# Six gate/up chunks of the first feed-forward half as seven block products, with their forms made earlier

## The chip, the cores and the metric

The kernel runs on one core of a Trainium2 chip. The metric is the device time of the program in microseconds (us), the median of several executions. Times "from the span's start" are those of one profiled execution, counted from its first instruction.

## The reference

The program is a block of a hybrid model on 528 tokens (16 meta tokens and 512 of the sequence) of width 1024: a feed-forward layer, a mixer (latent attention and a gated delta rule), a second feed-forward layer, and then a second block with two more attention branches. The change is in the first feed-forward layer alone:

```
D_FF = 2816
def rmsnorm(x, w):
    x32 = x.astype(jnp.float32)
    y = x32 * lax.rsqrt(jnp.mean(x32 * x32, axis=-1, keepdims=True) + EPS)
    return (y * w.astype(jnp.float32)).astype(x.dtype)
def swiglu(x, w_gate, w_up, w_down):
    return (jax.nn.silu(x @ w_gate) * (x @ w_up)) @ w_down
...
h = h + 0.5 * swiglu(rmsnorm(h, ffn1_norm[l]), ffn1_w_gate[l], ffn1_w_up[l], ffn1_w_down[l])
```

## The kernel before

**Precision.** Each product of two float32 matrices is made of three matmuls (`mm3`, L745 to L747): every operand is split into a high part (`WHI`, `UH`, `FH`, `GH`) and a low part, the difference (`WLO`, `UL`, `FL`, `GL`), and high x high, low x high and high x low are summed in PSUM. ScalarE makes a high part (a copy in the rounded type), VectorE the low part (source minus high).

**The stream of weights.** All weights come as chunks in one fixed order (`STREAM`), through two slots (`RAW[:, slot]`, slot = n % 2): SP loads chunk n, ScalarE makes `WHI` (`hi_part`, L1542), VectorE `WLO` (`lo_part`, L2125), TensorE multiplies and counts `mm_done`, VectorE reads PSUM and counts `evac`. The feed-forward layer takes two halves of 11 x 128 hidden columns: f1u0 (gate/up chunks n = 0 to 10, each the gate and the up columns of 128 hidden ones, 16 blocks of 128 x 128), f1d0 (down chunks 11 to 18, 11 blocks each), f1u1 (gate/up 19 to 29), f1d1 (down 30 to 37). Every engine has its own instruction queue and works through it in order; the helper `stream` calls a body per chunk, as a hardware loop of two chunks per turn, or straight (`straight=True`).

**A plain gate/up chunk** is 96 matmuls of 128 x 128 by 264 tokens (8 blocks of the width, gate and up, two token halves, three precision products). In its body (`up`), ScalarE and VectorE first make the weights of chunk n + 1 (`next_hi`, `next_lo`). Then they wait for chunk n's product: VectorE multiplies the gate by the row factors (L2351), ScalarE takes tanh (L1678), VectorE makes silu (L2353), multiplies by the up part out of PSUM (L2358, which counts `evac`) and by the row factors (L2361), ScalarE makes `GH` (L1680), VectorE `GL` (L2363).

**A seven-product chunk** (`seven_products`, `seven_up`; chunks 19 to 29) does the same product by Strassen's seven block products: the width, the hidden columns of gate and up, and the tokens are each cut in two. Seven combinations of the normed inputs are needed ("forms", 128 x 1056 each, `FH` and `FL`, made once) and seven combinations of the weights ("pieces" of 128 x 512, made per chunk: two sums for the lower half, `lower_sums`, two more in `piece_low`, and then high and low of each of the seven). A product is 12 matmuls of 264 tokens, so a chunk is 84. Some products are wanted in two outputs: ScalarE copies a PSUM half bank into another (`forked`, L1609, counts `snap`) or to `SNAP` (`copied`, L1616), TensorE waits for such copies before products 2, 4 and 6, and VectorE adds twice at the end. Pieces live in a ring of eight places in the two weight slots.

**The forms** are made in the down chunks 11 to 17 (`normed_inputs`, `forms`, `form_high`): eight normed halves (L2164), two differences (L2173, L2176) and seven low parts (L2187, L2185) by VectorE, seven high parts (L1563) by ScalarE, two sums by POOL (L639, L641). TensorE waits for all seven (`f_lo`) before the first product of the first seven-product chunk.

**Memory.** `FH`, `FL`, `XB` (the forms before the split) and `UH0`, `UL0` (the plain normed inputs) share an arena by their life times.

Of the kernel before, what the change touches and what calls it, by code (L numbers as in the profile page):

```python
# [17 lines left out]
P = 128  # L18
# [4 lines left out]
HT = T1 // 2  # L23
# [4 lines left out]
FP = 272  # L28
# [51 lines left out]
def build(nc, io):  # L80
# [44 lines left out]
    def region(start, *items):  # L125
# [14 lines left out]
    FH, FL, SNAP, SX, TANH1, SILU1, GF1, GH, GL, _ = region(  # L140
        arena, ("FH", [P, 7, 4, FP], f32r), ("FL", [P, 7, 4, FP], f32r), ("SNAP", [P, 1, HT], f32),
        ("SX", [P, PIECE], f32), ("TANH1", [P, 2, T1], f32), ("SILU1", [P, 2, T1], f32), ("GF1", [P, 2, T1], f32),
        ("GH", [P, FHALF, T1], f32r), ("GL", [P, FHALF, T1], f32r))
    XB, _ = region(arena + size([P, 7, 4, FP]), ("XB", [P, 8, 4, FP], f32))
    UH0, UL0, _ = region(arena, ("UH0", [P, KD, T1], f32r), ("UL0", [P, KD, T1], f32r))
# [300 lines left out]
    SEVEN_RUNS = (range(START["f1u1"], START["f1u1"] + FHALF),)  # L446
# [8 lines left out]
    FORM_HI = (0, 1, 5, 2, 3, 4, 6)  # L455
# [15 lines left out]

    def piece_place(t, n, i):

        where = RING[(7 * (n - SEVEN_FIRST[n]) + i) % 8]
        return t[:, where // 4, where % 4 * PIECE:(where % 4 + 1) * PIECE]

    def piece_free(eng, n, i):

        q = 7 * (n - SEVEN_FIRST[n]) + i
        if q < 8:  # L480
            eng.wait_ge(mm_done, SEVEN_FIRST[n] - (1 if q < 4 else 0))
        else:
            eng.wait_ge(p_mm, 7 * SEVEN[SEVEN_FIRST[n]] + q - 7)
# [10 lines left out]
    def hidden(f):  # L494
        return (GHS, GLS) if f else (GH, GL)
# [77 lines left out]
    def _(sp):  # L573
# [40 lines left out]
        for name in ORDER[:-1]:  # L614
            stream(sp, name, load(name), straight=name == "f1u1", first=2 if name in ("f1d0", "f1d1") else 0)
            if name == "z":
                spread_rows()
# [122 lines left out]
    def _(pe):  # L740
# [13 lines left out]
        def square_sums(v):  # L754
# [59 lines left out]
        def down_by_halves(n, slot, gh, gl):  # L814

            for half in range(2):
                if half:
                    pe.wait_ge(evac, n)
                for k in range(FHALF):
                    if half == 0:  # L820
                        pe.wait_ge(gl_rdy, 3 * FHALF + k + 1)
                    a = HS * half
                    last = mm3(PS[:, 1 - half, 0:HS], slot, k * P, gh[:, k, a:a + HS], gl[:, k, a:a + HS],
                               k == 0, k == FHALF - 1)
# [25 lines left out]
        def ffn(f, c0, w):  # L850
            hi, lo = parts(3 * f)
            gh, gl = hidden(f)
            for half in range(2):
# [27 lines left out]
                def down(n, j, turn, slot, nxt):  # L881
                    pe.wait_ge(lo_rdy, n + 2)
                    pe.wait_ge(evac, n - 1)
                    if last_down(f, half, j):
                        down_by_halves(n, slot, gh, gl)
                        return
                    for k in range(FHALF):
                        pe.wait_ge(gl_rdy, (2 * f + half) * FHALF + k + 1)
                        for b, (a, m, c) in enumerate(pieces(w)):
                            last = mm3(PS[:, 4 * slot + b, c:c + m], slot, k * P, gh[:, k, a:a + m],  # L890
                                       gl[:, k, a:a + m], k == 0, k == FHALF - 1)
# [4 lines left out]
                stream(pe, f"f{f + 1}u{half}", up, straight=f == 0 and half == 1, first=2)  # L896
# [633 lines left out]
    def _(act):  # L1530
# [24 lines left out]
        def form_high(i):  # L1555
# [5 lines left out]
            else:  # L1561
                act.wait_ge(xn_rdy, 4 if i == 0 else KD)
# [48 lines left out]
        def copied(n):  # L1611
# [3 lines left out]
            act.wait_ge(comb, 2 * c)  # L1615
            A(SNAP[:, 0, :], bank_half(n, 1), ACT.Copy).then_inc(snap, 1)  # L1616

        def hidden_high(n, q, j):

            act.wait_ge(evac, n + 1)  # L1620
            A(GH[:, j, :], GF1[:, q % 2, :], ACT.Copy).then_inc(gh_rdy, 1)

        def seven_up(n, j, q, nxt):
# [7 lines left out]
            if first:  # L1631
# [15 lines left out]
            if not last:  # L1647
# [8 lines left out]
        def ffn(f, c0, w):  # L1656
            TANH, SILU, GF = staging(f)
            for half in range(2):
                m0 = f * FJ + half * FHALF - START[f"f{f + 1}u{half}"]

                def up(n, j, turn, slot, nxt):
# [18 lines left out]
                    A(hidden(f)[0][:, j, 0:w], GF[:, slot, 0:w], ACT.Copy).then_inc(gh_rdy, 1)  # L1680

                def down(n, j, turn, slot, nxt):
                    next_hi(n, turn, slot, nxt)
                    if f == 0 and half == 0:
                        for i in {2: FORM_HI[:3], 3: FORM_HI[3:5], 4: FORM_HI[5:]}.get(j, ()):
                            form_high(i)
# [6 lines left out]
                stream(act, f"f{f + 1}u{half}", up, straight=f == 0 and half == 1, first=2)  # L1693
                stream(act, f"f{f + 1}d{half}", down, straight=f == 0 or half == 1)
# [20 lines left out]
        for k in range(KD):  # L1715
            A(SQ[:, k, :], H[:, k, :], ACT.Square).then_inc(sq_rdy, 1)
# [394 lines left out]
    def _(dve):  # L2111
# [32 lines left out]
        def lower_sums(n):  # L2144
# [45 lines left out]
        def hidden_low(q, j):  # L2190

            dve.wait_ge(gh_rdy, q + 1)
            TT(GL[:, j, :], GF1[:, q % 2, :], GH[:, j, :].bitcast(f32), ALU.subtract).then_inc(gl_rdy, 1)

        def seven_up(n, j, q, nxt):
# [6 lines left out]
            else:  # L2202
                hidden_low(q - 1, j - 1)
            if last:
# [13 lines left out]
            if not last:  # L2218
# [11 lines left out]
            else:  # L2230
# [59 lines left out]
        def normed_inputs(j):  # L2290

            if j == 0:
                dve.wait_ge(mm_done, FHALF)
            for k in range(4 * j, 4 * j + 4) if j < 2 else ():
                normed_halves(k)
# [32 lines left out]
        def ffn(f, c0, w):  # L2328
            gh, gl = hidden(f)
            TANH, SILU, GF = staging(f)  # L2330
            for half in range(2):
# [3 lines left out]
                def up(n, j, turn, slot, nxt):  # L2335
# [6 lines left out]
                    elif n == 0:  # L2342
                        lo_part(2, 0, SLOT)
                    if f == 1:
# [18 lines left out]
                    TT(gl[:, j, 0:w], GF[:, slot, 0:w], gh[:, j, 0:w].bitcast(f32),  # L2363
                       ALU.subtract).then_inc(gl_rdy, 1)

                def down(n, j, turn, slot, nxt):
# [12 lines left out]
                    if f == 0 and half == 0:  # L2379
                        normed_inputs(j)  # L2380
# [4 lines left out]
                    if f == 0 and half == 0:  # L2385
                        forms(j)
# [949 lines left out]
```

## Time and profile before

| | us |
|---|---|
| median of 3 runs (1556.37 to 1559.57) | 1557.88 |
| the profiled execution | 1557.85 |
| its span, first to last instruction | 1556.2 |
| TensorE busy | 1519.9 |
| VectorE busy | 955.3 |
| ScalarE busy | 593.6 |

The profiled execution's mean granted TensorE clock is 0.997. Busy time of TensorE is that of pipelined instructions, which overlap: one row of 0.28 us for a matmul of 264 tokens does not mean that it holds the engine for that long; the distance from one to the next does.

### The profile page before, as it was taken

Reading aid. Unit: us, or ns where it says so; the run is one execution under the profiler, and the core shown is the slowest. Engines: PE = TensorE matmul, PEld = TensorE weight load, DVE = VectorE, ACT = ScalarE, POOL = GpSimd, SP = SyncE. Lnnn points to the kernel's source line nnn. Section 1 sums busy time; section 2 is a strip of 40 time slices with the busy share of each in tenths; the row PEclk is TensorE's granted clock in tenths of the full one; section 3 lists DMA queues with packets and bytes.
Section 4 is the critical chain, followed back from the end, with each engine's and each line's share of the span. In section 5 each row is a group of like instructions: output and inputs, shape, how many; then the busy total and the mean of one; then the engine's idle time right before and its main releaser. Section 6 shows DMA issues by size and latency. Waiting matters only on the chain.

```text
span 1556.2 us, 30392 instructions
## 1 busy us (share of the span) xinstructions
PE 1519.9 (98%) x12676; PEld 1334.2 (86%) x12676; DVE 955.3 (61%) x1528; ACT 593.6 (38%) x968; POOL 127.0 (8%) x124
## 2 busy tenths in 40 slices
PE   9999999999999989999999989999999989999998
PEld 8999999999997779988888868888888877776777
DVE  6546588855389776546345666634666565557872
ACT  6222356632255562043223312212222143446960
POOL 0000100000001640500000000000000000000410
PEclk9999999999999999999999999999999999999999
DMA  6222223246332200012224243333342353211001
GB/s 242 81 99 75 92 100 109 92 114 145 96 85 70 61 3 31 5 42 81 94 90 166 82 162 127 131 119 123 134 153 76 106 213 135 76 47 55 2 13 71
DMA packets 27679, 147.85 MB, mean 95 GB/s; under 512 B 2928, under 2 KB 3328, under 8 KB 16944
## 3 DMA queue, kind: packets, MB, share of 16 engines
q1 hardware_dynamic: 21616, 122.50, 22.5%
q0 software_dynamic: 5424, 22.68, 5.3%
q8 instruction: 84, 1.38, 0.4%
q10 hardware_dynamic: 528, 1.08, 0.2%
q14 instruction: 27, 0.22, 0.0%
HBM read 140.97 MB, written 5.27 MB: 94 GB/s over the span
## 4 chain that ended last, share of the span: by engine, by line
PE 87%; DVE 7%; ACT 3%; issue 2%; DMA 1%; POOL 1%; DVEq 0%; SPq 0%; ACTq 0%; POOLq 0%
PE PS L745 22%; PE PS L746 22%; PE PS L747 22%; PE PS L845 2%; PE PS L847 2%; PE PS L846 2%; PE PS L1262 1%; PE PS L1197 1%; PE PS L1157 1%; PE PS L1247 1%; PE PS L1260 1%; ACT PB L1900 1%; PE PS L781 1%; DVE WLO L2125 1%; PE PS L1070 1%
## 5 line engine op out<-in xcount | busy, mean ns | idle before, releaser
L1542 ACT ACTIVATE WHI<-RAW 128x2048 fp32r<-128x2048 f32 (+3 forms) x113 | 189.4, 1676 | 276.2 <-PE PS L747 272.4
L2125 DVE TENSOR_TENSOR WLO<-RAW,WHI 128x2048 fp32r<-128x2048 f32 (+3 forms) x113 | 226.0, 2000 | 65.9 <-ACT WHI L1542 65.2
L745 PE MATMUL PS<-UH,WHI 128*128 128x264 f32 (+1 forms) x736 | 226.9, 308 | 2.1 <-DVE WLO L2125 2.1
L746 PE MATMUL PS<-UH,WLO 128*128 128x264 f32 (+1 forms) x736 | 225.7, 307 | 0.0
L747 PE MATMUL PS<-UL,WHI 128*128 128x264 f32 (+1 forms) x736 | 225.4, 306 | 0.0
L745 PE MATMUL PS<-UHS,WHI 128*128 128x512 f32 x520 | 205.6, 395 | 5.5 <-DVE WLO L2125 5.5
L746 PE MATMUL PS<-UHS,WLO 128*128 128x512 f32 x520 | 203.4, 391 | 0.0
L747 PE MATMUL PS<-ULS,WHI 128*128 128x512 f32 x520 | 203.4, 391 | 0.0
L745 PEld LDWEIGHTS PS<-UH,WHI 128*128 128x128 f32 x736 | 138.5, 188 | 9.1 <-DVE WLO L2125 2.5
L746 PEld LDWEIGHTS PS<-UH,WLO 128*128 128x128 f32 x736 | 138.4, 188 | 6.4 <-issue 0.2
L747 PEld LDWEIGHTS PS<-UL,WHI 128*128 128x128 f32 x736 | 138.2, 188 | 6.3
L745 PEld LDWEIGHTS PS<-UHS,WHI 128*128 128x128 f32 x520 | 98.3, 189 | 27.9 <-issue 7.2
L747 PEld LDWEIGHTS PS<-ULS,WHI 128*128 128x128 f32 x520 | 98.2, 189 | 20.8
L746 PEld LDWEIGHTS PS<-UHS,WLO 128*128 128x128 f32 x520 | 98.4, 189 | 20.3 <-issue 0.2
L746 PE MATMUL PS<-GH,WLO 128*128 128x264 f32 x352 | 100.3, 285 | 0.0
L747 PE MATMUL PS<-GL,WHI 128*128 128x264 f32 x352 | 100.0, 284 | 0.0
L745 PE MATMUL PS<-GH,WHI 128*128 128x264 f32 x352 | 99.9, 284 | 0.0
L1678 ACT ACTIVATE TANH<-SILU 128x512 f32<-128x512 f32 (+1 forms) x33 | 21.0, 637 | 190.8 <-DVE SILU L2351 190.8
L845 PE MATMUL PS<-FH,WHI 128*128 128x264 f32 x308 | 87.8, 285 | 0.1
L847 PE MATMUL PS<-FL,WHI 128*128 128x264 f32 x308 | 87.3, 283 | 0.0
L846 PE MATMUL PS<-FH,WLO 128*128 128x264 f32 x308 | 87.3, 283 | 0.0
L2383 DVE SCALAR_TENSOR_TENSOR H<-PS,H 128x528 f32<-128x528 f32 (+2 forms) x31 | 21.6, 698 | 95.8 <-PE PS L747 95.8
(474 smaller groups left out, 3241.2 us busy)
## 6 DMA issues: line engine op xcount, KB each, us to landing
RAW<-in_f2u SPq DMA_DIRECT2D x22, 1024.0 KB, 4.8
RAW<-in_f1u SPq DMA_DIRECT2D x21, 1024.0 KB, 4.8
ADA<-in_ada POOLq DMA_DIRECT2D x24, 512.0 KB, 4.7
RAW<-in_f1d SPq DMA_DIRECT2D x16, 704.0 KB, 4.1
RAW<-in_f2d SPq DMA_DIRECT2D x16, 704.0 KB, 4.1
RAW<-in_wi SPq DMA_DIRECT2D x10, 1024.0 KB, 4.8
RAW<-in_w SPq DMA_DIRECT2D x8, 1024.0 KB, 5.4
RAW<-in_mg SPq DMA_DIRECT2D x8, 1024.0 KB, 4.8
```

The costliest lines, as they stand in the source:

```text
L745: mm(out, WHI[:, slot, c:c + w], hi, start=first, stop=False)
L746: mm(out, WLO[:, slot, c:c + w], hi, start=False, stop=False)
L747: return mm(out, WHI[:, slot, c:c + w], lo, start=False, stop=last)
L781: out = mm(PS[:, 2 * which + b, c:c + m], stationary[:, 0, (which * KD + k) * P:(which * KD + k + 1) * P], moving[:, k, a:a + m], start=fi ...
L845: mm(out, whi[:, ks], hi, start=starts and k == 0, stop=False, skip_group_check=True)
L846: mm(out, wlo[:, ks], hi, start=False, stop=False, skip_group_check=True)
L847: last = mm(out, whi[:, ks], lo, start=False, stop=ends, skip_group_check=True)
L1070: last = mm(scores(i, p, k0, k1), q, KH[0:96, h, k0:k1], start=True, stop=True)
L1542: A(WHI[:, slot, 0:w], RAW[:, slot, 0:w], ACT.Copy).then_inc(hi_rdy, 1)
L1678: A(TANH[:, slot, 0:w], SILU[:, slot, 0:w], ACT.Tanh, scale=0.5).then_inc(tanh_rdy, 1)
L2125: TT(WLO[:, slot, 0:w], RAW[:, slot, 0:w], WHI[:, slot, 0:w].bitcast(f32), ALU.subtract).then_inc(lo_rdy, 1)
L2383: STT(h, psum(4 * slot, w), 0.25, h, ALU.mult, ALU.add)\
```

## The change

Chunks 5 to 10 of f1u0 become seven-product chunks too (`PLAIN = 5` stay plain). The forms are now made in the bodies of the plain chunks 1 to 4 and serve both halves: in chunk 1 the eight normed halves, in 2 the differences, in 2, 3 and 4 the low parts (`LOWS_IN`), the high parts in 1, 2 and 3 (`HIGHS_IN`), all ahead of the wait for that chunk's own product. `forms` and `normed_inputs` are gone from the down chunks. f1u0 is written straight on all engines, while f1d0 gets loops on ScalarE and VectorE. In the memory, `FL` is written over the forms it is made from, `FH` starts where `XB`'s last form lies, and the hidden parts are in two tiles (`GHA` for chunks 0 to 4, `GHB` for 5 to 10, over `UH0`), chosen by `hidden(f, part, j)`; `SNAP` and `SX` lie over the plain chunks' staging, so their first use waits for those chunks. The last chunk of the run (10) makes its pieces 5 and 6 late, in its own body, in places that its own products 0 and 1 have left, so that chunk 11's weights find their slot.

```
-FP = 272
+FP = 264
+PLAIN = 5
...
-    SEVEN_RUNS = (range(START["f1u1"], START["f1u1"] + FHALF),)
+    SEVEN_RUNS = (range(START["f1u0"] + PLAIN, START["f1u0"] + FHALF), range(START["f1u1"], START["f1u1"] + FHALF))
...
-    FORM_HI = (0, 1, 5, 2, 3, 4, 6)
+    FORM_HI = (1, 5, 4, 0, 3, 2, 6)
+    HIGHS_IN = {1: (1, 5), 2: (4, 0, 3), 3: (2, 6)}
+    LOWS_IN = {2: (5, 4), 3: (1, 0, 3, 2), 4: (6,)}
...
+    def late_pieces(n):
+        return ends_run(n) and n < START["f1u1"]
+    def piece_back(n, i):
+        return 5 if late_pieces(n) and i >= 5 else 8
     def piece_place(t, n, i):
-        where = RING[(7 * (n - SEVEN_FIRST[n]) + i) % 8]
+        where = RING[(7 * (n - SEVEN_FIRST[n]) + i - piece_back(n, i)) % 8]
...
 # ScalarE
-                act.wait_ge(xn_rdy, 4 if i == 0 else KD)
+                act.wait_ge(xn_rdy, KD)
+            if i == 0:
+                act.wait_ge(fs_rdy, 1)
+                act.wait_ge(fd_rdy, 1)
...
                     elif n == 0:
                         hi_part(2, 0, 1, SLOT)
+                    for i in HIGHS_IN.get(n, ()) if isinstance(n, int) else ():
+                        form_high(i)
...
 # copied(n)
+            if c == 0:
+                act.wait_ge(silu_rdy, n)
...
 # VectorE
-        def forms(j):
-            if j == 2:
+        def forms(n):
+            if n == 1:
+                for k in range(KD):
+                    normed_halves(k)
+            if n == 2:
                 form_differences(4)
                 form_differences(2)
-            for i in range(2 * j - 6, min(2 * j - 4, 7)) if 3 <= j < 7 else ():
+            for i in LOWS_IN.get(n, ()):
                 form_low(i)
...
                     elif n == 0:
                         lo_part(2, 0, SLOT)
+                    if f == 0:
+                        forms(n)
                     if f == 1:
                         modulation(q, slot, turn, m0 - FJ)
                     dve.wait_ge(mm_done, n + 1)
```

## Rows read from the trace of the kernel before

**Rows 1.** The page's first part: busy us (share of the span) xinstructions.
```profile
PE 1519.9 (98%) x12676; PEld 1334.2 (86%) x12676; DVE 955.3 (61%) x1528; ACT 593.6 (38%) x968; POOL 127.0 (8%) x124
```
**Rows 2.** Table by stage: stage, length, busy of each engine (xcount), PEclk, DMA, GB/s.
```profile
34.00:80.00 46.00, 46.00 (x383) 46.00 (x382) 23.32 (x24) 12.40 (x12) 0.00 (x0) 1.00 0.22 75
203.50:316.00 112.50, 112.37 (x926) 112.12 (x926) 95.42 (x157) 69.11 (x139) 0.00 (x0) 1.00 0.29 101
```
**Rows 3.** Timeline, evictions and the end of f1u0: start, us, engine, line, operation, [idle before].
```profile
45.78 0.71 DVE L2351 TENSOR_TENSOR SILU<-PS,KEEP 128x528 f32<-128x528 f32 x1 [3.14 <-PE PS L747]
...
126.80 0.71 DVE L2351 TENSOR_TENSOR SILU<-PS,KEEP 128x528 f32<-128x528 f32 x1 [2.91 <-PE PS L747]
...
138.28 0.81 PE L803 MATMUL PS<-TAB,RELB 32*16 32x383 f32 x2
...
215.14 0.70 DVE L2224 SCALAR_TENSOR_TENSOR GF<-PS,SILU 128x528 f32<-128x528 f32 x1
...
285.57 0.70 DVE L2224 SCALAR_TENSOR_TENSOR GF<-PS,SILU 128x528 f32<-128x528 f32 x1
```
**Rows 4.** Timeline of VectorE and ScalarE in chunk 1's body and after.
```profile
33.22 0.71 DVE L2363 TENSOR_TENSOR GL<-GF,GH 128x528 fp32r<-128x528 f32 x1 [0.71 <-ACT GH L1680]
34.11 0.71 DVE L2351 TENSOR_TENSOR SILU<-PS,KEEP 128x528 f32<-128x528 f32 x1 [0.18 <-PE PS L747]
...
38.43 0.71 DVE L2363 TENSOR_TENSOR GL<-GF,GH 128x528 fp32r<-128x528 f32 x1 [0.71 <-ACT GH L1680]
40.35 2.29 DVE L2125 TENSOR_TENSOR WLO<-RAW,WHI 128x2048 fp32r<-128x2048 f32 x1 [1.21 <-ACT WHI L1542]
...
34.85 0.65 ACT L1678 ACTIVATE TANH<-SILU 128x528 f32<-128x528 f32 x1 [1.67 <-DVE SILU L2351]
...
38.31 1.90 ACT L1542 ACTIVATE WHI<-RAW 128x2048 fp32r<-128x2048 f32 x1
```
**Rows 5.** Timeline of the form work in the down chunks, on VectorE, ScalarE and POOL.
```profile
145.52 2.81 DVE L2164 SCALAR_TENSOR_TENSOR XB<-H,COL,KEEP 128x528 f32<-128x528 f32 x4
...
164.06 1.25 DVE L2173 TENSOR_TENSOR XB<-XB 128x1056 f32<-128x1056 f32 x1
...
172.06 2.42 DVE L2187 TENSOR_TENSOR FL<-XB,FH 128x1056 fp32r<-128x1056 f32 x2
...
156.73 3.02 ACT L1563 ACTIVATE FH<-XB 128x1056 fp32r<-128x1056 f32 x3
...
166.68 3.79 POOL L641 TENSOR_TENSOR XB<-XB 128x1056 f32<-128x1056 f32 x1 [10.60 <-DVE XB L2176]
```
**Rows 6.** Timeline around chunk 19, the first seven-product chunk: VectorE, ScalarE, TensorE.
```profile
197.32 0.69 DVE L2154 TENSOR_TENSOR SX<-RAW 128x512 f32<-128x512 f32 x1
...
202.63 0.69 DVE L2142 TENSOR_TENSOR RAW<-RAW 128x512 f32<-128x512 f32 x1
...
205.27 1.66 ACT L1553 ACTIVATE WHI<-RAW 128x512 fp32r<-128x512 f32 x3
...
203.33 0.28 PE L845 MATMUL PS<-FH,WHI 128*128 128x264 f32 x1
...
212.39 0.39 PE L845 MATMUL PS<-FH,WHI 128*128 128x264 f32 x1
...
213.96 0.28 PE L845 MATMUL PS<-FH,WHI 128*128 128x264 f32 x1
```
**Rows 7.** The page's sixth part, DMA issues: KB each, median us to landing.
```profile
RAW<-in_f1u SPq DMA_DIRECT2D x21, 1024.0 KB, 4.8
```
**Rows 8.** Timeline of TensorE at two longer stands, and the table by stage there.
```profile
467.25 0.39 PE L745 MATMUL PS<-UH,WHI 128*128 128x264 f32 x1 [1.95 <-DVE WLO L2125]
...
915.39 0.77 PE L745 MATMUL PS<-UHS,WHI 128*128 128x512 f32 x1 [5.33 <-DVE WLO L2125]
...
463.00:470.00 7.00, 5.05 (x41) 4.84 (x41) 6.73 (x11) 2.00 (x2) 0.00 (x0) 1.00 0.21 68
...
915.40:921.20 5.80, 5.80 (x14) 4.54 (x15) 4.01 (x7) 1.87 (x3) 0.53 (x1) 0.51 0.72 267
```

More of the change, by code:

```diff
@@ L492, in place_free, with hidden @@
             eng.wait_ge(mm_done, n - 1)
-    def hidden(f):
-        return (GHS, GLS) if f else (GH, GL)
+    def hidden(f, part, j):
+        if f:
+            return (GHS, GLS)[part][:, j, :]
+        return ((GHA, GLA)[part][:, j, :] if j < PLAIN else (GHB, GLB)[part][:, j - PLAIN, :])
     def runs(b):
@@ L614, in _ @@
         for name in ORDER[:-1]:
[L615 removed]
+            stream(sp, name, load(name), straight=name in ("f1u0", "f1u1"), first=2 if name in ("f1d0", "f1d1") else 0)
             if name == "z":
@@ L822, in down_by_halves @@
                     a = HS * half
-                    last = mm3(PS[:, 1 - half, 0:HS], slot, k * P, gh[:, k, a:a + HS], gl[:, k, a:a + HS],
-                               k == 0, k == FHALF - 1)
+                    last = mm3(PS[:, 1 - half, 0:HS], slot, k * P, hidden(1, 0, k)[:, a:a + HS],
+                               hidden(1, 1, k)[:, a:a + HS], k == 0, k == FHALF - 1)
                     if half and k == 7:
@@ L895, in ffn @@
                     pe.wait_ge(rev_rdy, 1)
-                stream(pe, f"f{f + 1}u{half}", up, straight=f == 0 and half == 1, first=2)
+                stream(pe, f"f{f + 1}u{half}", up, straight=f == 0, first=2)
                 if f == 0 and half == 0:
@@ L1646, in seven_up @@
             forked(n, 1, 4)
-            if not last:
+            if not last and not late_pieces(n + 1):
                 piece_high(n + 1, 5)
@@ L1679, in up @@
                     act.wait_ge(gf_rdy, q + 1)
-                    A(hidden(f)[0][:, j, 0:w], GF[:, slot, 0:w], ACT.Copy).then_inc(gh_rdy, 1)
+                    A(hidden(f, 0, j)[:, 0:w], GF[:, slot, 0:w], ACT.Copy).then_inc(gh_rdy, 1)
                 def down(n, j, turn, slot, nxt):
                     next_hi(n, turn, slot, nxt)
-                    if f == 0 and half == 0:
-                        for i in {2: FORM_HI[:3], 3: FORM_HI[3:5], 4: FORM_HI[5:]}.get(j, ()):
-                            form_high(i)
                     if half == 1 and j == 0:
@@ L1691, in down @@
                         high(1, j)
-                stream(act, f"f{f + 1}u{half}", up, straight=f == 0 and half == 1, first=2)
-                stream(act, f"f{f + 1}d{half}", down, straight=f == 0 or half == 1)
+                stream(act, f"f{f + 1}u{half}", up, straight=f == 0, first=2)
+                stream(act, f"f{f + 1}d{half}", down, straight=half == 1, first=0 if f else 2)
         def only_weights(n, j, turn, slot, nxt):
@@ L2217, in seven_up @@
             TT(both, SNAP[:, 0, :], both, ALU.add).then_inc(comb, 1)
-            if not last:
+            if not last and not late_pieces(n + 1):
                 piece_low(n + 1, 5)
@@ L2391, in down @@
                             low(1, j)
-                stream(dve, f"f{f + 1}u{half}", up, straight=f == 0 and half == 1, first=0 if half else 2)
+                stream(dve, f"f{f + 1}u{half}", up, straight=f == 0, first=0 if half else 2)
                 if f == 0 and half == 0:
@@ L2396, in ffn @@
                     TS(REV, PS[0:16, 7, 0:383], -1.0, None, ALU.mult).then_inc(rev_rdy, 1)
-                stream(dve, f"f{f + 1}d{half}", down, straight=f == 0 or half == 1)
+                stream(dve, f"f{f + 1}d{half}", down, straight=half == 1, first=0 if f else 2)
         V.memset(CST[:, 1:2], EPS * EPS)
```

63 lines of the change are left out of this document (29 added, 34 removed).

## The prediction

> **What bounds the kernel now.** The page's first part says TensorE is busy for 98% of the span [rows 1]. So a microsecond off the matrix work is a microsecond off the end, unless TensorE then has to wait. The table by stage says how near the other engines are to the limit [rows 2]. In 46 us of plain gate/up chunks VectorE is busy for half the time. In the 112.5 us of the eleven chunks that are already done with seven products it is busy for 95.4, so it has hardly any slack to give.
>
> The change lies in the first 145 us, and there the order of each engine's queue decides. I number chunks from 0: gate/up 0 to 10, down 11 to 18, gate/up 19 to 29. A plain chunk takes 11.57 us ((126.80 - 45.78)/7) and a seven-product chunk 10.06 by VectorE's evictions ((285.57 - 215.14)/7) [rows 3]. TensorE's own figure is a little more: a plain chunk is 96 matmuls at 0.1205 us, so 84 take 10.12. The first half's last plain chunk is over at 138.2, just before the small L803 matmul [rows 3].
>
> **What is removed.** Six chunks (5 to 10) drop 12 of 96 matmuls each: 6 x (11.57 - 10.12) = 8.7 us off TensorE. In the down chunks the form work goes away, but VectorE and ScalarE had room there, and TensorE did not wait; I price that at nothing. Chunk 19 keeps its order of steps and its small stand (it waits at 212.39 for ScalarE's copy, where 72 matmuls after 203.33 would be 212.0), so nothing there either [rows 6].
>
> **What is added, on one chain.** The forms (8 normed halves, 2 differences, 7 low parts on VectorE; 7 high parts on ScalarE; 2 sums on POOL) are now made in the bodies of chunks 1 to 4, ahead of the eviction of that chunk's own product. The next chunk but one gets its high and low weights only behind that eviction and the hidden part that follows it. In the kernel before this goes, for chunk 1: L2351 at 34.11, TANH 34.85, WHI of chunk 3 at 38.31, WLO at 40.35, done at 42.64; TensorE wants it at 45.6 [rows 4]. The slack is 3.0 us. Now body by body, in the times of the kernel before.
>
> Body 1. VectorE is free at 33.85, after GL of chunk 0 [rows 4] (a following instruction starts some 0.08 before the one ahead ends, as the row of four at 145.52 has it; I take that throughout). Eight normed halves at 0.68 (four before the next instruction at +2.72 [rows 5]) are 5.44: 39.29. ScalarE starts its two high parts on their signal; three take 3.02 [rows 5], so two end by 41.4, and TANH, queued behind them, goes at 41.37 where it went at 34.85. That is 6.5 later. WLO of chunk 3 starts at 46.88 and ends at 49.17. TensorE stands from 45.6 to 49.2: 3.6 us.
>
> Body 2. Behind that WLO (next instruction at 49.09) come two differences (1.25 each, 2.46 with the hand-over between them) and two low parts (2.42 for two, 1.17 each to the next) [rows 5]: L2351 of chunk 2 at 53.89. ScalarE's three high parts (3.02) run beside them from 50.4 to 53.4. From L2351 to WLO is 6.24 (40.35 - 34.11) [rows 4]: WLO of chunk 4 from 60.13 to 62.4. TensorE has done chunk 3 at 49.2 + 11.57 = 60.8 and stands 1.6 us.
>
> Body 3. Four low parts from 62.34, 4.68: L2351 of chunk 3 at 67.02, and to GL 4.32 (38.43 - 34.11) [rows 4], with 0.63 to the next: 71.97.
>
> Body 4. The sums and the first four pieces of chunk 5 take, as at 197.32 to 202.63, 5.31 and one more step of 0.61 [rows 6]: 77.89. Then the seventh low part, 1.25, and the first product waits for that one (its wait for all seven forms): TensorE starts chunk 5 at 79.1. It was through with chunk 4 at 62.4 + 11.57 = 74.0 and stands 5.1 us.
>
> Chunk 5. VectorE evicts chunk 4 only now: L2351 at 79.06. ScalarE's copy of its hidden part goes at 82.7; behind it stand the fifth piece (0.55) and the copy that forks product 0 in PSUM, at 83.8, and product 2 waits for that fork. It would want it at 79.1 + 2.9 = 82.0. From here the queues hold what they hold in chunk 19, where the three high pieces start at 205.27 [rows 6]; now they start at 84.12, which is 121.15 earlier. So product 6 goes at 212.39 - 121.15 = 91.24, and chunk 6 at 213.96 - 121.15 = 92.81 [rows 6]. Chunk 5 has taken 13.7 us in place of 10.12: 3.6 lost. Chunks 6 to 10 then go at the pace of chunks 20 to 24, 5 x 10.12: the first half's gate/up ends at 92.8 + 50.6 = 143.4, where it ended at 138.2. The hand-over to the down chunks needs two late pieces, made behind products 0 and 1 and wanted from product 5; chunk 11's weights go to places that chunk 9 has left. Neither is late by these durations.
>
> Waits priced at nothing, with their cover: the load of chunk 5 starts when chunk 3's low weights are done (49.2) and takes 4.8 [rows 7], and is first read at 71.2; POOL's forms take at most 3.79 [rows 5], the first from 39.4 and the second from 51.6, and ScalarE wants them at 51 and 61. If POOL took twice as long the first would still be in time. Straight code in place of loops: bound 0 to 1 us on either side; I take 0, since TensorE has no idle time in either kind of stretch [rows 2].
>
> **Sum.** Stands 3.6 + 1.6 + 5.1 + 3.6 = 13.9, less 8.7, is 5.2, as the two end points give, 143.4 - 138.2. The profiled execution took 1557.85 us (span 1556.2 and 1.65 around it), which is also the median of the runs shown: 1557.85 + 5.2 = 1563.1 us. Each step leans on rows good to a few hundredths, some forty of them, and the unrolled bodies may differ from looped ones by a tenth each: plus or minus 1.5 for the mechanism alone.
>
> **The clock.** The trace has the same thing later: at 915.39 TensorE had stood 5.33 us for a WLO, and the granted clock was 0.51 (nearly all at the 1.2 GHz level) through 915.4 to 921.2 [rows 8]; 5.8 us at half speed cost 2.9. After 1.95 us of idle time at 467.25 the clock stayed at 1.00 [rows 8]. My stands are 3.6 and 5.1, between the two. The Trainium skill (TensorE: Matmul & The Clock Gate, "HAM oscillation — how this bites in real kernels") has it that a long enough idle gap puts the clock back to its lower level, and that this returns with every such gap; this speaks against a change that opens gaps, and the trace agrees at 915.4. By that rule both longer stands are dear. By the chain above most of it is absorbed: if chunk 3 runs slow for some us, it ends at 63.7 and the next stand is gone in its place, and after the 5.1 stand products 0 and 1 would only reach the fork, at 84.9, that they wait for anyway (84.2). So I put it at 0 to 3 us, and nearest 0.
>
> **Rivals.** (a) The cover holds: VectorE is half idle in plain chunks, the forms disappear in it, and only the gain is seen, less the 0.5 us that chunk 19 also loses (213.96 - 203.33 is 10.63 [rows 6]): 1557.85 - 8.7 + 0.5 = 1549.7. For it: some 5.7 us of idle VectorE per chunk ((46 - 23.3)/4 [rows 2]). Against it: that idle time lies after WLO and before the eviction's start, while the added work delays a chain with 3.0 us of slack. It decides for "faster" only if the added delay of bodies 1 to 3 stays under that. 7%. (b) Half of it: TANH and the eviction slip in ahead in bodies 2 and 3, so that the second stand and most of the loss in chunk 5 fall away, 3.6 + 5.1 + 0.5 - 8.7 = +0.5: 1558.4. 7%. (c) The forecast, 1563.1, 74%. (d) The clock falls after the 5.1 us stand and stays down into products 2 to 6, so that the 2.9 us above are paid in full: 1566.0. 12%.
>
> **Chances and range.** About 0.2% (3.1 us) is what a measurement here can tell from no change. Faster by more: (a) and a sliver of (b), 0.08. Within: most of (b) and the low tail of (c), 0.10. Slower by more: 0.82. The range takes (c) with its 1.5, the three runs' own spread of about 1.6, and (d): 1560.2 to 1566.6.
>
> **What would show it.** In the profile after: TensorE's waits have a row for WLO at L2125 with stands near 49.2 and 62.4 of about 3.6 and 1.6, a stand of about 5 before the first L845 matmul near 79, and one of some 2 us for ScalarE's PSUM copy (L1609 before) near 84; VectorE's first L2351 gap filled by eight XB instructions; the L803 matmul near 143.4. From there to the end everything is later by the same 5.2. It is wrong if TensorE shows no stand in 45 to 85, or if L803 comes before 138.2; and a step is wrong if the stands add up but the seven-product chunks 6 to 10 take more than 10.2 us each.

## The result and the profile after

The kernel after takes 1568.24 us (median of 7 runs, 1565.6 to 1575.12), the kernel before beside it on the same chip 1558.01 (7 runs, 1556.37 to 1560.04): ratio 1.0064, 95% interval 1.0052 to 1.0077, so 10.2 us slower. Slower was forecast, but with half of that, 5.2 us; 1568.24 lies above the range. The profiled execution of after took 1568.25 us, its span is 1566.5 against 1556.2. I go by that pair.

First the page's first part for after (busy us, share of the span, xinstructions) and the table by stage: the 46 us of plain chunks of [rows 2], and 50 us out of chunks 19 to 29.

```profile
PE 1518.9 (97%) x12604; PEld 1333.0 (85%) x12604; DVE 977.5 (62%) x1582; ACT 614.7 (39%) x1028; POOL 126.7 (8%) x124
...
34.00:80.00 46.00, 37.33 (x292) 36.71 (x290) 37.13 (x42) 16.71 (x19) 5.89 (x2) 0.96 0.13 47
...
250.00:300.00 50.00, 50.00 (x411) 50.00 (x411) 45.03 (x75) 31.88 (x65) 0.00 (x0) 1.00 0.31 106
```

The columns of the table are the stage, its length, the busy time of TensorE, of its weight loads, of VectorE, ScalarE and POOL (xinstructions), the granted clock, the DMA share and GB/s. TensorE has 72 matmuls less and is still busy for nearly the same time as in [rows 1]: 1518.9 us for 12,604 matmuls against 1519.9 for 12,676. In the plain chunks it was idle for 8.7 of 46 us, where it had no idle time in [rows 2]; VectorE went from 23.3 us busy to 37.1.

A stand is a stretch in which TensorE waits for another engine. Next come all of its waits in 34 to 150 (what it waited for: us in total, times, longest), and then TensorE's timeline (start, us, line, operation, [idle before]):

```profile
PE PS L763 <- DVE WLO L2146: 5.4, 2, 3.5
PE PS L863 <- DVE FL L2207: 4.9, 1, 4.9
```
```profile
49.45 0.39 PE L763 MATMUL PS<-UH,WHI 128*128 128x264 f32 x1 [3.46 <-DVE WLO L2146]
...
64.85 0.39 PE L763 MATMUL PS<-UH,WHI 128*128 128x264 f32 x1 [1.96 <-DVE WLO L2146]
...
81.64 0.56 PE L863 MATMUL PS<-FH,WHI 128*128 128x264 f32 x1 [4.88 <-DVE FL L2207]
...
93.53 0.40 PE L863 MATMUL PS<-FH,WHI 128*128 128x264 f32 x1
...
146.55 0.81 PE L821 MATMUL PS<-TAB,RELB 32*16 32x383 f32 x2
```

The three stands are where they were forecast, and almost as long: 3.46, 1.96 and 4.88 for 3.6, 1.6 and 5.1. What is off is when they come. The product that was to start at 91.24 starts at 93.53, 2.29 late, and the relative rows (the small matmul from `RELB` that follows the first half's gate/up chunks: L821 now, L803 in [rows 3]), forecast for 143.4, start at 146.55: 8.27 after the 138.28 of before in place of 5.2. The fourth stand, some 2 us near 84 for ScalarE's fork in chunk 5, did not show: TensorE went through products 0 and 1 at half clock and began product 2 at 87.06, when the copy (86.11, 0.37 us) was already done. VectorE in bodies 1, 2 and 4, with POOL's instructions last:

```profile
34.22 5.52 DVE L2184 SCALAR_TENSOR_TENSOR XB<-H,COL,KEEP 128x528 f32<-128x528 f32 x8
39.65 0.70 DVE L2371 TENSOR_TENSOR SILU<-PS,KEEP 128x528 f32<-128x528 f32 x1
...
47.10 2.29 DVE L2146 TENSOR_TENSOR WLO<-RAW,WHI 128x2048 fp32r<-128x2048 f32 x1 [1.09 <-ACT WHI L1559]
49.31 1.25 DVE L2193 TENSOR_TENSOR XB<-XB 128x1056 f32<-128x1056 f32 x1
50.60 1.26 DVE L2196 TENSOR_TENSOR XB<-XB 128x1056 f32<-128x1056 f32 x1
51.77 4.69 DVE L2207 TENSOR_TENSOR FL<-XB,FH 128x1056 fp32r<-128x1056 f32 x2
...
56.38 0.69 DVE L2371 TENSOR_TENSOR SILU<-PS,KEEP 128x528 f32<-128x528 f32 x1
...
80.24 1.25 DVE L2207 TENSOR_TENSOR FL<-XB,FH 128x1056 fp32r<-128x1056 f32 x1
81.41 0.70 DVE L2371 TENSOR_TENSOR SILU<-PS,KEEP 128x528 f32<-128x528 f32 x1
...
39.82 2.49 POOL L657 TENSOR_TENSOR XB<-XB 128x1056 f32<-128x1056 f32 x1 [39.25 <-DVE XB L2184]
...
51.93 3.41 POOL L659 TENSOR_TENSOR XB<-XB 128x1056 f32<-128x1056 f32 x1 [9.63 <-DVE XB L2196]
```

The row to look at is that of two low parts at 51.77: 4.69 us, where two took 2.42 in [rows 5]. The line's own figures (L2207) give 1.25 for one and 3.52 for the other. The second starts at 52.94, while POOL's sum runs from 51.93 to 55.34, and ends at 56.46: 1.12 after POOL's end, about its own 1.25. POOL's other sum, at 39.82, lies beside an eviction that reads PSUM, and delays nothing (0.70 at 39.65 is what such an eviction takes elsewhere).

Last, the granted clock, as a share of the full 2.4 GHz (stage, length, TensorE busy (xmatmuls), PEclk, DMA share, GB/s):

```profile
50.30:53.70 3.40, 3.40 (x18) 0.54 0.83 308
53.70:81.00 27.30, 21.10 (x172) 1.00 0.12 40
81.00:87.80 6.80, 6.16 (x29) 0.52 0.00 0
```

TensorE ran near its 1.2 GHz level for 3.4 us after the 3.46 stand and for 6.8 us at the end of the 4.88 stand; after 1.96 the clock stayed at 1.00.

### The profile page after: what moved, and what is told of

Same layout as the page of the kernel before. It is cut to its first block, busy times and chain, and to the rows that moved or that the text cites. A ratio compares the mean times of both kernels' runs of the same rounds, so it can differ in the third digit from the quotient of the medians.

```text
span 1566.5 us, 30390 instructions
## 1 busy us (share of the span) xinstructions
PE 1518.9 (97%) x12604; PEld 1333.0 (85%) x12604; DVE 977.5 (62%) x1582; ACT 614.7 (39%) x1028; POOL 126.7 (8%) x124
## 4 chain that ended last, share of the span: by engine, by line
PE 84%; DVE 8%; ACT 4%; issue 2%; DMA 1%; POOL 1%; DVEq 0%; SPq 0%; ACTq 0%; POOLq 0%
PE PS L763 20%; PE PS L764 19%; PE PS L765 19%; PE PS L863 4%; PE PS L864 4%; PE PS L865 4%; PE PS L1214 1%; PE PS L1279 1%; PE PS L1174 1%; PE PS L1264 1%; PE PS L1277 1%; DVE WLO L2146 1%; PE PS L1087 1%; PE PS L799 1%; ACT PB L1921 1%
## 5 line engine op out<-in xcount | busy, mean ns | idle before, releaser
L763 PE MATMUL PS<-UH,WHI 128*128 128x264 f32 (+1 forms) x544 | 174.1, 320 | 7.6 <-DVE WLO L2146 7.6
L764 PE MATMUL PS<-UH,WLO 128*128 128x264 f32 (+1 forms) x544 | 172.6, 317 | 0.0
L765 PE MATMUL PS<-UL,WHI 128*128 128x264 f32 (+1 forms) x544 | 172.3, 317 | 0.0
L863 PE MATMUL PS<-FH,WHI 128*128 128x264 f32 x476 | 137.2, 288 | 5.1 <-DVE FL L2207 4.9
L864 PE MATMUL PS<-FH,WLO 128*128 128x264 f32 x476 | 136.8, 287 | 0.0
L865 PE MATMUL PS<-FL,WHI 128*128 128x264 f32 x476 | 136.7, 287 | 0.0
L863 PEld LDWEIGHTS PS<-FH,WHI 128*128 128x128 f32 x476 | 90.9, 191 | 5.8 <-issue 5.1
L865 PEld LDWEIGHTS PS<-FL,WHI 128*128 128x128 f32 x476 | 91.0, 191 | 0.0
L864 PEld LDWEIGHTS PS<-FH,WLO 128*128 128x128 f32 x476 | 90.8, 191 | 0.0
L2154 DVE TENSOR_TENSOR WLO<-RAW,WHI 128x512 fp32r<-128x512 f32 x102 | 68.4, 686 | 13.7 <-ACT WHI L1570 13.7
```

Source lines behind the costliest of these rows:

```text
L763: mm(out, WHI[:, slot, c:c + w], hi, start=first, stop=False)
L764: mm(out, WLO[:, slot, c:c + w], hi, start=False, stop=False)
L765: return mm(out, WHI[:, slot, c:c + w], lo, start=False, stop=last)
L863: mm(out, whi[:, ks], hi, start=starts and k == 0, stop=False, skip_group_check=True)
L864: mm(out, wlo[:, ks], hi, start=False, stop=False, skip_group_check=True)
L865: last = mm(out, whi[:, ks], lo, start=False, stop=ends, skip_group_check=True)
```

## Theories

A: the stands come from work on VectorE's queue, one engine in order, and the 3.1 us beyond the forecast are a term each for (1) VectorE's low part that waits for POOL, 2.3, and (2) slower matmuls in the seven-product chunks, 0.7 to 0.9. Rivals: B, the low part is slow for another reason, such as being written over its own source; D, the granted clock after the stands carries the loss; and for the pace, P, the forms' new row pitch (1056 bytes, was 1088), against Q, the larger load beside it.

## Experiments

**1. POOL's second sum on VectorE.** The forms of after, but form 6 is made by VectorE in body 2.

```diff
 # POOL
-        pool.wait_ge(fd_rdy, 2)
-        G2(form(6), form(2), form(1), ALU.subtract).then_inc(fs_rdy, 1)
 # VectorE, body 2, behind the two differences
+                TT(form(6), form(2), form(1), ALU.subtract).then_inc(fs_rdy, 1)
```

> The changed kernel with POOL's second sum (form 6) made by VectorE in chunk 2's body instead. Theory A (a VectorE instruction with two SBUF inputs stands still while POOL's two-input instruction runs: in the changed kernel one low part took 3.52 us in place of 1.25, ending 1.1 us after POOL's ended): both low parts take 1.25 again, 2.27 us come back and 1.2 are added, so chunk 2's eviction starts at about 55.3 instead of 56.4 and the small L803 matmul at about 145.5 instead of 146.6; about 1 us faster than the changed kernel. Rival B (the low part was slow for another reason, such as being written over its own source): it stays at 3.5 us, and everything is 1.2 us later than in the changed kernel.

Measured: 1566.67 us, ratio to before 1.0045 (1.0032 to 1.0059). VectorE has one instruction more, and is earlier for it once the later start of this run is taken off:

```profile
53.73 1.26 DVE L2321 TENSOR_TENSOR XB<-XB 128x1056 f32<-128x1056 f32 x1
54.91 2.42 DVE L2205 TENSOR_TENSOR FL<-XB,FH 128x1056 fp32r<-128x1056 f32 x2
...
147.43 0.81 PE L819 MATMUL PS<-TAB,RELB 32*16 32x383 f32 x2
```

The two low parts take 2.42 again. This run began 1.85 late (its first eviction at 33.28 against 31.43 in after, with the clock near half from 11.6 to 15.0), so its relative rows come 0.97 earlier than after's, counted from there; A said 1.07. 

**2. No sum on POOL or VectorE.** Form 6 is a copy of form 2 made by ScalarE, so product 7 multiplies other values; all else is after.

```diff
-        G2(form(6), form(2), form(1), ALU.subtract).then_inc(fs_rdy, 1)
 # ScalarE, ahead of high part 2
+                            A(XB[:, 6, :, 0:HT], XB[:, 2, :, 0:HT], ACT.Copy).then_inc(fs_rdy, 1)
```

> The changed kernel with form 6 left out: ScalarE copies form 2 into its place in chunk 3's body (so the seventh product is of other data), POOL does nothing there and VectorE nothing more. Theory A: the low part of 3.52 us takes 1.25, chunk 2's eviction starts at about 54.1, all that follows up to L803 is 2.3 us earlier (144.3), and the time is 2.3 us below the changed kernel's, about 1566. Rival B: nothing moves by more than 0.3 us.

Measured: 1564.89 us, ratio 1.004 (1.0026 to 1.0053).

```profile
51.53 2.42 DVE L2209 TENSOR_TENSOR FL<-XB,FH 128x1056 fp32r<-128x1056 f32 x2
53.87 0.70 DVE L2373 TENSOR_TENSOR SILU<-PS,KEEP 128x528 f32<-128x528 f32 x1
...
144.07 0.81 PE L819 MATMUL PS<-TAB,RELB 32*16 32x383 f32 x2
```

Body 2's eviction is at 53.87, where the prediction had 53.89, and the relative rows are 2.48 earlier (2.25 with the 0.23 by which the run began earlier). So the 2.27 us by which one VectorE instruction waited for POOL's come through whole to the relative rows. The medians differ by 3.35, with intervals of about 2 us on each.

**3. No form work, fills by ScalarE.** The form work is left out, and ScalarE fills the fourteen forms with copies of H.

```diff
-    HIGHS_IN = {1: (1, 5), 2: (4, 0, 3), 3: (2, 6)}
-    LOWS_IN = {2: (5, 4), 3: (1, 0, 3, 2), 4: (6,)}
+    FILLS_IN = {2: range(4), 3: range(4, 9), 4: range(9, 14)}
```

> The changed kernel with the form work of VectorE and POOL left out: ScalarE, idle there, fills the fourteen form tiles with copies of the input (so the seven-product chunks multiply other data). This is the gain term by itself. Theory A (all of the loss is VectorE's form work on the chain): TensorE does not stand in 45 to 75, chunk 5 loses at most 1 us, L803 comes at about 138.2 - 8.5 + 0.5 = 130.3, and the time is about 8 us below the kernel before, 1550. Rival C (the seven-product chunks in the first half are themselves dearer than 10.2 us, or their hand-over to the down chunks stands): L803 comes later than 132 even so.

Measured: 1556.92 us, ratio 0.9986 (0.9977 to 0.9995); the relative rows at 136.61, not the 130.3 expected. That is beyond the rival's 132, but by a fault of the experiment's own: five fills stood behind the pieces in body 4, and chunk 5 waited 2.81 us for them. The granted clock was near half for the first 6.0 us of the chunk; no wait followed there that could take it up, so it cost about 3 us more (an estimate from the half speed). TensorE's stand, and the clock behind it:

```profile
72.17 0.56 PE L858 MATMUL PS<-FH,WHI 128*128 128x264 f32 x1 [2.81 <-ACT FL L1688]
...
72.20:78.20 6.00, 6.00 (x27) 0.50 0.00 0
```

**4. The halves a body later.** All eight normed halves and the first two high parts in body 2, so that body 1 is as before.

```diff
-            if n == 1:
+            if n == 2:
                 for k in range(KD):
                     normed_halves(k)
```

> The changed kernel with the eight normed halves and the first two high parts moved one body later, behind chunk 1's eviction. Theory A (VectorE's queue from 34 to 95 us has next to no idle time, so only its total length counts): the 3.5 us stand before chunk 3 goes, the one before chunk 4 grows from 2 to about 6 us, and L803 moves by only about -1.2 us, what TANH of chunk 1 no longer waits for; 1567. Rival D (each stand is set by its own stage's slack of 3 us, as the prediction's first step put it, and a stand that is avoided is won): 3.5 us are won, L803 at 143.

Measured: 1569.06 us, ratio 1.0062 (1.0048 to 1.0075); relative rows at 148.02, 1.47 later than in after, where 1.2 earlier was expected. That is far from the 143 of the rival in this expectation, which is another D than the one above. The stand before chunk 3 is gone, as A had it, and the one before chunk 4 has grown, to 8.43 us where about 6 was expected. VectorE, POOL and TensorE:

```profile
49.94 3.41 DVE L2196 TENSOR_TENSOR XB<-XB 128x1056 f32<-128x1056 f32 x1
...
53.27 4.68 DVE L2207 TENSOR_TENSOR FL<-XB,FH 128x1056 fp32r<-128x1056 f32 x2
...
48.69 3.54 POOL L657 TENSOR_TENSOR XB<-XB 128x1056 f32<-128x1056 f32 x1 [48.12 <-DVE XB L2184]
...
53.43 3.41 POOL L659 TENSOR_TENSOR XB<-XB 128x1056 f32<-128x1056 f32 x1 [1.20 <-DVE XB L2196]
...
66.32 0.59 PE L763 MATMUL PS<-UH,WHI 128*128 128x264 f32 x1 [8.43 <-DVE WLO L2146]
```

Both of POOL's sums now lie beside a VectorE instruction with two SBUF inputs, and each time the later one pays: a difference of 1.26 takes 3.41 (to 53.35; POOL ended at 52.23, 1.12 before), a low part again 3.5. For experiment 4 that is 2.2 us more than in after, and -1.2 + 2.2 = +1.0 is near the measured 1.47 (1.15 from the run's own start).

**5. No form work, fills spread.** Experiment 3 with five fills by ScalarE in each of bodies 2 and 3, two by VectorE in each, none in body 4.

```diff
+    FILLS_IN = {2: range(5), 3: range(5, 10)}
+    VFILLS_IN = {2: range(10, 12), 3: range(12, 14)}
```

> The kernel after without the form work: VectorE's normed halves, differences and low parts and POOL's sums are left out, and the fourteen forms hold copies of H instead, ten made by ScalarE (five each in bodies 2 and 3) and four by VectorE (two each in the same bodies), so that no body carries more than three steps of ScalarE beyond a plain one. It isolates what six more seven-product chunks bring. Theory A (the stands come from VectorE's added work alone): no stand of TensorE before chunk 5 of over 1 us; the relative-row matmul starts at 138.3 - 8.7 + 0.5 (the fork in chunk 5) + 0.8 (five chunks at 122.1 ns per matmul in place of 120.5) = about 131, and the time is about 1551 to 1552. Rival (seven-product chunks here bring less than 12 matmuls each): relative rows after 133, time above 1553.

Measured: 1553.91 us, ratio 0.9976 (0.9965 to 0.9986). So the six chunks do bring something once their forms cost nothing, but 4.5 us by the medians and 3.9 at the relative rows, not the 7.3 of A. Both numbers fall on the rival's side (after 133, above 1553), though not for its reason:

```profile
74.03 0.39 PE L860 MATMUL PS<-FH,WHI 128*128 128x264 f32 x1 [2.24 <-ACT PS L1626]
...
134.36 0.81 PE L817 MATMUL PS<-TAB,RELB 32*16 32x383 f32 x2
```

No wait for low weights or forms is left, and chunks 6 to 10 follow each other at TensorE's own 10.26 us. What remains is chunk 5's fork: ScalarE's copy stands behind the hidden part of chunk 4, 2.24 us, and the granted clock was near half for 3.4 us from 74.6, which costs about 1.7. With these two A's sum comes out (131 + 1.7 for the stand beyond the 0.5 priced + 1.7 = 134.4); that split is worked out, not shown by a run of its own. The forms' work thus costs 146.55 - 134.36 = 12.2 us more on the path than the fills that replace it here.

**6. The row pitch, in the kernel before.** One constant, which also moves the buffers behind the forms.

```diff
-FP = 272
+FP = 264
```

> The kernel before with one constant changed, the row pitch of the forms FH and FL from 272 to 264 elements (1088 to 1056 bytes), which also moves the buffers that lie behind them. Only chunks 19 to 29 read the forms. Theory P (the pitch, or the place that comes with it, sets the slower pace of seven-product chunks): a matmul in them goes from 121.1 to 122.1 ns, 11 chunks of 84 make +0.9 us, and the time is 0.5 to 1.5 us above the kernel before. Rival Q (the pace is set by the six runs more of these chunks, or by VectorE being busy beside them): 121.1 stays, time unchanged.

**7. The high forms' pitch, in the kernel after.** FH gets its 1088 bytes back, FL keeps 1056.

```diff
+FQ = 272
-    ... ("FH", [P, 7, 4, FP], f32r))
+    ... ("FH", [P, 7, 4, FQ], f32r))
```

> The kernel after with the row pitch of the high forms FH back at 272 elements, FL left at 264 (for both there is no room). Theory P: the pace in the seven-product chunks falls from 122.1 toward 121.4 ns per matmul, as FH is the moving operand of two of the three matmuls of a split product; over 17 chunks of 84 that is -1.0 us. Rival Q: 122.1 stays, time unchanged.

**8. The pitch with padding, in the kernel before.** As 6, with 1792 bytes behind FL, so that the buffers that follow stand as in before.

```diff
-FP = 272
+FP = 264
+    ("FPAD", [P, 448], f32)
```

> The kernel before with the forms' row pitch at 1056 bytes, and 1792 bytes of padding behind them, so that every buffer that follows stands where it stands in the kernel before; only FL and the pitch differ. Theory P1 (the pitch of the forms itself): the matmuls of chunks 19 to 29 take 122.1 ns as they do with the pitch of 1056 and no padding. Theory P2 (the place of the buffers behind them): 121.1 ns as in the kernel before. The time is within 1 us of the kernel before in both.

Measured: 1559.17 us for 6, ratio 1.0007 (0.9998 to 1.0016), so not told apart from before by time; 1567.41 for 7, ratio 1.0056 (1.0042 to 1.0069), not told apart from after; one run of 8, 1560.23. The trace tells more. In 250 to 300 TensorE never idles at a clock of 1.00, so the number of matmuls is the pace (columns as above): before, then 6, then 7, then 8.

```profile
250.00:300.00 50.00, 50.00 (x415) 1.00 0.30 103
```
```profile
250.00:300.00 50.00, 50.00 (x412) 1.00 0.29 98
```
```profile
250.00:300.00 50.00, 50.00 (x411) 1.00 0.30 105
```
```profile
250.00:300.00 50.00, 50.00 (x411) 1.00 0.28 97
```

415 against 411 or 412 is 120.5 against 121.5 ns; taken from start to start of neighbouring matmuls it is 121.1 before and 122.1 to 122.3 in after and in 6, 7 and 8. Evictions in that stretch are 10.18 apart before (295.69 to 305.87) and 10.26 in 6 (296.46 to 306.72). Q falls: one constant in the kernel before slows its seven-product chunks by 1 ns a matmul, and with the padding too, so it isn't the place of the buffers behind. But P as I had it, by FH, falls as well: FH alone at 1088 bytes gives nothing back, in contrast to the 121.4 expected. What is common to all slow ones is FL at 1056 bytes, but in each of them it also begins at another place than in before, and XB's pitch changed too. FL's pitch alone doesn't fit well either. Start to start, the three matmuls of a split product (FH with WHI, FH with WLO, FL with WHI) take 121.4, 120.9 and 121.0 ns before, 122.1, 121.9 and 122.3 in 6 and 8, but 123.2, 122.5 and 121.1 in 7, where those on FL have the pace of before and those on FH don't. Which part of the layout it is stays open.

**9. TensorE kept busy in the stands.** Idle matmuls ahead of two waits.

```diff
+                    if isinstance(n, int) and n == 3:
+                        pe.wait_ge(evac, n - 1)
+                        keep_busy(5)
...
+            if c == 0:
+                keep_busy(7)
```

> The kernel after with five idle matmuls of 0.5 us put before TensorE's wait for chunk 3's low weights and seven before its wait for the forms in chunk 5, so that TensorE is not idle in the two long stands; their results are used by nobody. Theory A (the half clock after the stands falls into stretches that later waits absorb): the granted clock is 1.00 from 45 to 95, the relative rows stay within 0.6 us of 146.5, and the time within 1 us of the kernel after. Rival D (the clock after the stands costs what 3.4 and 6.8 us at half speed lose): the relative rows come 1.7 to 5 us earlier, and the time falls by as much.

Measured: 1567.0 us, ratio 1.0047 (1.0032 to 1.0063), relative rows at 146.67 against 146.55.

```profile
45.00:64.70 19.70, 16.26 (x116) 1.00 0.16 54
64.70:68.10 3.40, 3.13 (x14) 0.50 0.63 188
68.10:95.00 26.90, 25.36 (x181) 1.00 0.15 56
```

The clock stayed up after both filled stands, and fell after the one not filled (3.48 us before chunk 4 here), against my "1.00 from 45 to 95". Nothing was gained: as predicted, the slow stretches of after end in waits for VectorE and ScalarE. D falls for this part of the program, with one reserve: the idle matmuls ran up to 0.7 us past the forms (chunk 5's first product at 82.34 against 81.64), so about as much clock loss could be hidden in the tie.

**10. Seven products from chunk 7, forms thin.** Four chunks more instead of six; forms in bodies 1 to 6, all by VectorE; ScalarE's Silu in place of tanh and of one VectorE operation in the plain chunks; FH's pitch at 1088 bytes and two tables loaded later, to make room. So several things change at once.

```diff
-    HIGHS_IN = {1: (1, 5), 2: (4, 0, 3), 3: (2, 6)}
-    LOWS_IN = {2: (5, 4), 3: (1, 0, 3, 2), 4: (6,)}
+SEVENS_AT = 7
+    HIGHS_IN = {3: (1, 5, 4), 4: (0, 3, 2), 5: (6,)}
+    LOWS_IN = {4: (5, 1, 4), 5: (0, 3, 2), 6: (6,)}
```

> A version of the kernel after with the forms' work spread thin: chunks 7 to 10 go as seven products instead of 5 to 10; the forms are made in bodies 1 to 6, all by VectorE, never more than four steps in a body; the plain chunks of the first layer use ScalarE's Silu in place of a tanh and a VectorE operation, so VectorE has one operation less per chunk ahead of the hidden part; FH's pitch is 272; two rotary tables are loaded later, their place holds one hidden part. Theory A (a body's added work on VectorE costs what it exceeds the slack of 3 us): every body stays under or near its slack, stands together 1 to 2 us, four chunks bring 4 x 1.45 = 5.8, less 0.5 for the fork in chunk 7 and 0.5 for the pace: relative rows at 134.5 to 136.5 against 138.3, and the time 1555.5 to 1557.5. Rival (any forms' work in plain chunks stands out in full, about 25 us of steps against 11.6 us chunks): relative rows at 140 or later, time above 1559.

Measured: 1557.39 us, ratio 0.9992 (0.9983 to 1.0001). The relative rows at 136.03, inside the 134.5 to 136.5 of A; TensorE waits nowhere in the plain chunks, and 2.0 us for the fork in chunk 7.

```profile
66.20 3.59 DVE L2219 TENSOR_TENSOR FL<-XB,FH 128x1056 fp32r<-128x1056 f32 x3
69.71 0.70 DVE L2386 TENSOR_TENSOR SILU<-PS,KEEP 128x528 f32<-128x528 f32 x1
...
136.03 0.81 PE L830 MATMUL PS<-TAB,RELB 32*16 32x383 f32 x2
```

2.25 us are won at the relative rows, and the slower pace takes part of that back in chunks 19 to 29 (11 x 0.09 = 1.0): the medians are 1.0 apart, the interval just reaches 1.

**11. Seven products from chunk 6.** The same, packed into bodies 1 to 5.

```diff
+SEVENS_AT = 6
+    HIGHS_IN = {2: (1, 5), 3: (4, 0, 3), 4: (2, 6)}
+    LOWS_IN = {3: (5, 1), 4: (4, 0, 3, 2), 5: (6,)}
```

> The version with seven-product chunks from 7 on moved one chunk earlier: chunks 6 to 10 go as seven products, the forms are made in bodies 1 to 5, all by VectorE and never more than 4.8 us of them in a body (six halves; two halves and two differences; two sums and two low parts; four low parts; the last low part). Theory A (a body's own steps take about 6.4 us of VectorE there, so added work up to some 4.8 us fits into the 11.6 us of a plain chunk and costs nothing): one chunk more brings 12 matmuls, 1.3 us at the slower pace: relative rows near 134.7 against 136.0 with four chunks, and the time about 1556.1, some 0.15% below the kernel before. Rival (the bodies are full, 4.8 us stands out): a stand of TensorE of 1 us or more ahead of chunk 5 or 6, relative rows at 136 or later, time 1557.4 or more.

Measured: 1559.64 us, ratio 1.0002 (0.9993 to 1.0011); relative rows at 139.64, the rival's side. There is no stand ahead of chunk 5 or 6, though, but inside chunk 6:

```profile
61.54 0.70 DVE L2386 TENSOR_TENSOR SILU<-PS,KEEP 128x528 f32<-128x528 f32 x1
...
73.81 0.70 DVE L2386 TENSOR_TENSOR SILU<-PS,KEEP 128x528 f32<-128x528 f32 x1
...
89.48 0.59 PE L872 MATMUL PS<-FH,WHI 128*128 128x264 f32 x1 [5.43 <-ACT PS L1638]
```

The body with four low parts lasts 73.81 - 61.54 = 12.3 us on VectorE, longer than TensorE's 11.57. In 10 a body with three lasts 11.1 (58.62 to 69.71). Less the low parts (4.68 and 3.51 from start to start), both are 7.6: VectorE's steps plus its short waits for TANH, the hidden part and WHI. I had said 6.4, so the room in a body was 4.0 us and not the 4.8 that I filled. Against the 134.7 expected the relative rows are 4.9 late: 5.4 less the 2.0 that experiment 10 waits as well, and about 1.7 for a granted clock near half from 89.5, the stand's end, to 93.0. VectorE fell behind body by body, no chunk waited for it as long as its weights were there, and the whole delay came due at the first place where ScalarE's fork stands behind VectorE's eviction. No version that computes the block's own result beats before by more than can be measured here; experiments 3 and 5 do (0.9986 and 0.9976), but their forms hold other data.

## Why the prediction was wrong

**Right.** The mechanism and its places: the forms' work goes ahead of the eviction in the bodies, the low weights of chunks 3 and 4 come late (3.46 and 1.96 us), the seventh form holds chunk 5 (4.88), and slower by over 0.2%. The eight halves, the differences and the steps between eviction and WLO took what the rows said, to 0.15; body 2's eviction, with the POOL sum gone (experiment 2), is at 53.87 for 53.89. Rival (a) would have needed no stands; rival (b)'s +0.5 is far off. The clock near 0, against rival (d): its slow stretches ended in waits, and experiment 9 shows nothing to win there. That is no rule: where no wait came behind it, the slow clock was paid for (experiments 3, 5 and 11).

**The step that failed** is body 2: "two low parts (2.42 for two, 1.17 each to the next)". They took 4.69, for POOL's second sum lay beside them. The prediction asked of POOL only whether its forms come in time ("If POOL took twice as long the first would still be in time"), and not what it does to VectorE. The row was there: POOL's sum in the down chunks has 3.79 us in [rows 5], far above the 2.49 that it takes alone at 39.82, because it began 0.16 after a WLO of 1.62 us on VectorE and had to wait for it: the WLO ended at 168.14 and the sum at 170.47, 2.33 later. I read the 3.79 as POOL's own price. The kernel before also has VectorE paying: at 488.81 four of its instructions with two SBUF inputs take turns with four of POOL's. The first takes 0.68 and each other about 1.7.

```profile
166.52 1.62 DVE L2125 TENSOR_TENSOR WLO<-RAW,WHI 128x1408 fp32r<-128x1408 f32 x1
...
488.81 5.73 DVE L2588 TENSOR_TENSOR QH<-ROT 32x512 f32<-32x512 f32 x4
...
488.86 6.84 POOL L653 TENSOR_TENSOR QH<-ROT 32x512 f32<-32x512 f32 x4 [32.92 <-DVE ROT L2583]
```

The Trainium skill (GPSIMD Engine Reference, "Key points") says that POOL shares its SBUF interfaces with VectorE and that there is contention with VectorE instructions with two SBUF inputs; the trace agrees, at 4.69 for 2.42. The prediction had the eviction of chunk 2 (L2351 there, L2371 here) at 53.89; it was at 56.38, which is 2.49 late: 2.27 from POOL and 0.37 from a first eviction that much later in this execution, less 0.15, as body 1 took 5.36 from TANH to WLO and not 5.50. From there the queues carried it to product 6 (93.53 for 91.24, +2.29). That 2.29 is so near to 2.27 is in part luck, as the later start and the shorter steps cancel; the clean figure is the 2.25 of experiment 2. Experiments 1, 2 and 4 show it, by moving the sum, taking it away and doubling the overlap.

**The term that was mis-sized** is "6 x (11.57 - 10.12) = 8.7" for what is removed. A seven-product chunk at TensorE's own pace is 10.26 us here (chunks 7 to 10 begin at 105.43, 115.69, 125.95 and 136.21), so it is 6 x 1.31 = 7.9; 0.09 of each chunk came with the changed constant (experiments 6 and 8), the other 0.05 was in [rows 3] already, had I counted start to start (121.1 ns) and not taken the plain chunks' 120.5. From product 6 to the relative rows that is 53.02 us for 52.16 forecast, +0.86. So the prediction's own sign for a wrong step, more than 10.2 us for each of chunks 6 to 10, came. The diff changed FP, and the prediction passed over it. So 143.4 + 2.29 + 0.86 = 146.55, the measured start.

**"From there to the end everything is later by the same 5.2"**: no. The rest of the program is 2.03 longer (1566.5 - 146.55 against 1556.2 - 138.28). About 0.8 is the pace in chunks 19 to 29: ScalarE's forks are 8.44 late at the first (213.42 for 204.98) and 9.24 at the last (322.32 for 313.08). The other 1.2 isn't steady. Matmul by matmul, after is 9.49 behind before at 467.25, 10.96 at 470.65, 11.96 at 915.39, 10.88 at 921.08, 9.34 at 1270.99 and 10.36 at the last one (times of before). Most of these steps lie where the clock was near half in one of the two executions alone, or for longer in one; the first is this one, in after, where before kept 1.00 after 1.95 us [rows 8]:

```profile
476.74 0.59 PE L763 MATMUL PS<-UH,WHI 128*128 128x264 f32 x1 [1.98 <-DVE WLO L2146]
...
476.70:480.10 3.40, 3.36 (x15) 0.50 0.48 154
```

The stretches near half clock behind 138 sum to 10.2 us in both kernels, and the same remainder in experiments 5 to 11 is anywhere from 1417.7 to 1420.3, also in experiments 6 and 8, whose code is that of before but for the pitch, so I don't put it on the change.

## What to carry to other kernels

Before adding work to an engine whose busy share looks low, take its period per turn with the short waits in it (7.6 us in experiments 10 and 11, not the busy time), and allow only what is left of the bound engine's turn; a debt beyond that isn't seen at once, but at the next place where a queue joins. Keep POOL's instructions on SBUF away from VectorE's with two SBUF inputs, or give them to VectorE: doing POOL's sum on VectorE took 1.25 us and saved 2.27. A constant such as a row pitch is part of the change and wants its own price.

## What the runs showed of the hardware

- Of a VectorE and a POOL instruction that both read two SBUF operands, the one that starts later doesn't share with the other but waits for its end: 1.25 became 3.52 (after), 1.26 became 3.41 (experiment 4), each ending 1.12 after POOL's. It goes both ways: POOL's 2.49 became 3.41 (after), 3.54 (experiment 4) and 3.79 (before), each ending 2.3 after the VectorE instruction that ran when it started. I had expected a slowdown in proportion, if any.
- A stand of about 2 us can go either way. The clock stayed at 1.00 after 1.53 (experiment 10), 1.96 (after) and 1.95 (before, at 467.25); at the matching place in after it was near half for 3.4 us after 1.98. It was near half behind stands of 2.24 (experiment 5), 3.46 and 4.88 us.
- A slow stretch cost next to nothing where TensorE had to wait for another engine soon after (after; 146.67 for 146.55 in experiment 9), and about half its length where no wait came (1.7 us of 3.4 in experiment 5, an estimate).
- The same fp32 matmul of 264 columns takes 121.1 or 122.1 ns, start to start, by the layout of its moving operand's buffers (experiments 6 and 8).
